# Four places for landed weight tiles and four for their high halves, in place of five and three

## The reference

```python
for i in range(DEPTH):                                   # first block
    shift, scale, gate = jnp.split(cond @ ada_w[i] + ada_b[i], 3, axis=-1)
    h = rmsnorm(x, norm_g[i]) * (1.0 + scale) + shift
    ...
    o, oc = swa_mixer(...)  # i == 0: q, k, v, gate = h @ w_in; softmax; @ w_out
    o, oc = mla_mixer(...)  # i == 1: latents, w_qb, w_kvb; softmax; @ w_out
    x = x + gate * o
for i in range(DEPTH):                                   # second block
    h = pool_mixer(...) if i % 2 == 0 else dilated_attention(...)
    x = layer_norm(DEEPNORM_ALPHA * x + h, ln_mix_g[i], ln_mix_b[i])
    x = layer_norm(DEEPNORM_ALPHA * x + sqrelu_mlp(x, mlp_w_up[i], mlp_w_down[i]), ...)
```

## Time and profile before

| | |
|---|---|
| runs of the kernel before | 3536.13, 3531.57, 6973.23 us; median 3536.13 |
| profiled execution | 3533.72 us |
| its span, from the first to the last instruction | 3531.9 us |
| granted TensorE clock, mean over the span | 0.991 |
| weights read | 580 loads, 606.72 MB on their queue |

### The profile page before, as it was taken

The page is one execution under the profiler, slowest core; times in us unless marked ns, Lnnn a source line. Parts: engine busy times, 40 slices in busy tenths (PEclk is TensorE's granted clock), DMA queues, the critical chain, the costliest instruction groups (busy, mean ns, idle before and its releaser), DMA issues.

```text
span 3531.9 us, 43704 instructions
## 1 busy us (share of the span) xinstructions
PE 3443.9 (98%) x18399; PEld 2869.4 (81%) x18399; DVE 1907.8 (54%) x2689; ACT 1437.1 (41%) x1612; POOL 139.7 (4%) x78
## 2 busy tenths in 40 slices
PE   6999999999899999999999999999999999999999
PEld 3677777777799868878888888888998788888887
DVE  2453554633677855457544554464445675445555
ACT  3213334432455543535433443353344444334432
POOL 0000000000000000005000000040000050000000
PEclk9999999999999999999999999999999999999999
DMA  8743333354332374454555555545444455555553
GB/s 324 265 155 143 131 132 120 119 204 164 116 124 109 107 269 180 167 214 167 212 194 191 191 190 191 188 176 189 182 149 162 167 188 212 197 191 189 187 195 143
DMA packets 90848, 626.09 MB, mean 177 GB/s; under 512 B 10390, under 2 KB 11415, under 8 KB 17819
## 3 DMA queue, kind: packets, MB, share of 16 engines
q1 hardware_dynamic: 85536, 606.72, 47.0%
q10 hardware_dynamic: 5116, 16.57, 1.3%
HBM read 621.15 MB, written 2.10 MB: 176 GB/s over the span
## 4 chain that ended last, share of the span: by engine, by line
PE 93%; DVE 3%; ACT 1%; issue 1%; DMA 1%; SPq 0%; DVEq 0%; ACTq 0%
PE PS L630 15%; PE PS L518 14%; PE PS L519 14%; PE PS L524 14%; PE PS L639 8%; PE PS L573 4%; PE PS L580 4%; PE PS L574 4%; PE PS L664 2%; PE PS L654 2%; DMA raw<-in_weights 1%; PE PS L791 1%; PE PS L778 1%; PE PS L736 1%; PE PS L737 1%
## 5 line engine op out<-in xcount | busy, mean ns | idle before, releaser
L1739 DVE TENSOR_TENSOR wlo<-raw,whi 128x2048 fp32r<-128x2048 f32 (+1 forms) x484 | 1099.7, 2279 | 1068.7 <-ACT whi L1243 1060.5
L1243 ACT ACTIVATE whi<-raw 128x2048 fp32r<-128x2048 f32 (+1 forms) x484 | 908.5, 1885 | 1026.2 <-PE PS L524 591.3
L630 PE MATMUL PS<-xm,whi 128*128 128x512 f32 x2384 | 569.7, 391 | 0.8 <-DVE X L2199 0.8
L630 PEld LDWEIGHTS PS<-xm,whi 128*128 128x128 f32 x2384 | 437.9, 188 | 87.2 <-issue 1.6
L518 PE MATMUL PS<-whi,hid_hi 128*128 128x512 f32 x960 | 373.8, 389 | 0.0
L519 PE MATMUL PS<-whi,hid_lo 128*128 128x512 f32 x960 | 373.5, 389 | 0.0
L639 PEld LDWEIGHTS PS<-xm,wlo 128*128 128x128 f32 x2432 | 311.8, 191 | 11.9
L639 PE MATMUL PS<-xm,wlo 128*128 128x256 f32 x2432 | 315.4, 283 | 0.0
L524 PE MATMUL PS<-wlo,hid_hi 128*128 128x512 f32 x960 | 256.6, 389 | 0.0
L524 PEld LDWEIGHTS PS<-wlo,hid_hi 128*128 128x128 f32 x960 | 180.2, 188 | 37.4
L519 PEld LDWEIGHTS PS<-whi,hid_lo 128*128 128x128 f32 x960 | 180.2, 188 | 37.3
(11 more groups left out here) (369 smaller groups left out, 5278.7 us busy)
## 6 DMA issues: line engine op xcount, KB each, us to landing
raw<-in_weights SPq DMA_DIRECT2D x560, 1024.0 KB, 4.8
lnB<-in_ln ACTq DMA_DIRECT2D x4, 2048.0 KB, 9.5
raw<-in_weights SPq DMA_DIRECT2D x8, 768.0 KB, 4.1
X<-in_x SPq DMA_DIRECT2D x4, 1024.0 KB, 8.4
X<-in_x ACTq DMA_DIRECT2D x4, 1024.0 KB, 15.9
raw<-in_weights SPq DMA_DIRECT2D x8, 512.0 KB, 3.5
raw<-in_weights SPq DMA_DIRECT2D x4, 640.0 KB, 3.7
out_x<-X SPq DMA_DIRECT2D x8, 256.0 KB, 2.1
```

The source lines that it names most:

```text
L630: mm(PS[:, banks[ch // 2] + ch % 2, :], high_of(n, slice(c * PW + ch * P, c * PW + (ch + 1) * P)), x(4 * k + c).rearrange("p s t -> p (s t ...
L1243: return f(dst, src, ACT.Copy)
L1739: v.tensor_tensor(wlo[:, ring.place[n], 0:w], raw[:, ring.place[n], 0:w], whi[:, m % NH, 0:w], ALU.subtract).then_inc(lo_done, 1)
```

## The change

Both numbers change; their sum stays 8, so that every other array of the kernel stands where it did. There are now four places for landed tiles (their loads begin when the tile four places back is done, instead of five) and four for high halves (ACT may write a high half when the split tile four back is done, instead of three). `held` becomes four as well.

```diff
-NR, NH = 5, 3
+NR, NH = 4, 4
```

## The result

| | before | four and four |
|---|---|---|
| median | 3534.68 us (22 runs) | 3542.32 us (22 runs) |
| lowest and highest | 3530.97 and 3539.62 us | 3538.36 and 3546.69 us |
| profiled execution | 3533.72 us | 3546.43 us |
| its span | 3531.9 us | 3544.6 us |

The ratio is 1.0023, 95% interval [1.0017, 1.0029]: the change costs 6.0 to 10.2 us. One of the 22 runs of before took 6973.23 us; the ratio and the highest time in the table leave it out, and without it the median of before is 3534.17. The profiled execution of the changed kernel is one of its slowest ordinary runs.

A forecast was written before the change was run, and what follows sets the result against it. PE, busy 3443.9 of 3531.9 us, was taken as the bound. Start 4.0, MLA's end 3.1, clock 4.0 and tail -0.3 summed to 10.8 on the profiled 3533.72: 3544.5 us, range 3532 to 3558.

The forecast's parts named there:

- What bounds the kernel, and the steady part: PE bounds the kernel; in the MLPs later loads stay hidden and copies come 0.6 us earlier: value 0.
- ACT's waits for landings in the attention stages: Copies may wait for loads issued some 6 us later, but ACT and DVE have room: 0, at most 6 us.
- The start: Key/value stage's first step: PE waits for late loads of tiles 12, 13, 15, 16 and 17: +4.0 us.
- Later ada tiles of the stage: The 16 ada tiles in the key/value stage's later steps land in time: 0.
- MLA's end: After sixteen ada tiles in a row, the first tile of MLA's output projection lands late: PE +3.1 us.
- The clock: PE's longer waits drop the clock to half: 2.5 us at MLA's output projection, 1.5 at the start, +4.0 us.
- The tail: Final norm: DVE finishes its first block earlier, then waits for the second: -0.3 us.
- the ada streams run dry: Rival, chance 0.14: landings over 6.8 us exhaust two places for ada tiles; 3570 us at most, 3557 in the middle.
- nothing shows: Rival, chance 0.20: PE regains the start's waits later and the projection's load is faster; 3531 to 3537 us.
- the fourth high place pays: Rival, chance 0.04: ACT's extra room returns perhaps 20 of PE's 88 idle us: 3514 us.
- slower by over 2%: Rival, chance 0.02: the chain load, high, low, use sets the pace in MLPs and projections; 3734 us.

The follow-up runs named there:

- experiment 1: Four landed and three high places, against the kernel before with five and three: 3542.22 us, ratio 1.0028.
- experiment 4: Kernel before (five and three), all loads except the first 42 and 176 to 196 delayed as with four landed places: 3534.01 us, ratio 1.0004.
- experiment 8: Three landed and four high places, three held tiles, against the kernel before with five and three: 3710.96 us, ratio 1.0502.
- experiment 3: Kernel before (five and three), only loads 176 to 196, around MLA's end, delayed as with four landed places: 3535.74 us, ratio 1.0008.
- experiment 2: Kernel before (five and three), only the first 42 loads delayed as with four landed places: 3543.15 us, ratio 1.0025.
- experiment 5: Kernel before, four ada tiles moved ahead of the key/value stage, sixteen at MLA's end spread over three heads: 3521.64 us, ratio 0.9964.
- experiment 10: Kernel before, four ada tiles ahead of the key/value stage, no pairs in its first step, sixteen at MLA's end over three heads: 3520.91 us, ratio 0.9962.

## Why the prediction was right

The change was forecast 8.4 us over the median of before as then known; it costs 7.6 us by the medians. That these two are so near is luck in part. The sum was 10.8 us, on a profiled execution of 3533.72 us; the median of before was then 3536.13, from two ordinary runs, and came down to 3534.68 later. The 10.8 is what has to be compared. Step by step:

- **What bounds the kernel, and the steady part: right.** PE 70 of 70 us, ACT's waits turned from PE to loads, three and four high places equal (experiment 1), the other 517 loads without a cost that shows (experiment 4), and even three places cover the down projections, though not quite the up projections (experiment 8). The copy came 0.63 us earlier against PE for 0.6 forecast.
- **ACT's waits for landings in the attention stages: 0, right for four places.** PE is 9.9 us later than before at 170.72 us, behind the stage, and still some 10 us later at MLA's last ada tiles. With three places (experiment 8) these stages do lose time, and that the late copies are the reason was not tried.
- **The start: +4.0, measured 5.06** (6.12 less the 1.06 of before). Tile 12 cost 1.15 for 1.2 worked out, tile 13 1.61 for 1.4, tile 15 nothing for 0.7, tile 16 0.67 for 0.4. Tile 17 was mis-sized: 2.69 us of wait where I had 1.3, since its load was issued in the stretch from 80 to 81 us and took 7.3 us to land, for 5.6 in the earlier trace rows. The landings of 4.8, 5.6 and 6.5 us were too few to go by: at this place of the changed kernel a load that goes out when the queue is empty lands in 4.7 to 4.8 us, and one behind another in 6.7 to 7.3.
- **Later ada tiles of the stage: 0, right.** None waits in the changed kernel from 94 us on.
- **MLA's end: +3.1, measured 2.7** (a pause of 3.68 for 1.21, and 0.23 at the last ada tile); 3.0 in experiment 3. The sixteen themselves landed in time, but for those 0.2 us. With the pause, the waits named on loads and this one rose by 7.9 us, for the 25.3 to 33 forecast.
- **The clock: +4.0, measured about 3.1** in this profile: at most 2.1 at the start for 1.5 (small gaps included; its one new half-speed stretch accounts for up to 1.7), and 1.0 at MLA's end for 2.5, where I had priced the pause by one of 3.75 us with a half-speed stretch of 10 us behind it; here the stretch was 3.4 us.
- **The tail: -0.3, measured -0.2**, with DVE's idle time of 2.39 us where 2.4 was forecast.

The terms as measured sum to 5.06 + 2.7 + 3.1 - 0.2 = 10.7 us, for 10.8 forecast, and the ratio says 6.0 to 10.2. The profiles of experiments 1 to 3 have the same parts at +5.05 to +5.6 (stage, where this profile has 7.15) and +4.0 (MLA's end with its clock): 9.1 to 9.6. So my sum is probably 1 to 3 us too high for the median, and which term it is stays open: with the half-speed stretches shifting from run to run, these runs cannot settle it. Nor can they settle why experiment 2 costs 8.8 us by its ratio and 11.0 by its medians, more than the 5.05 in its profile; its interval reaches down to 4.9. The parts of experiments 2 to 4 sum to 0.0037, above the 0.0023 of the change, with errors of some 0.001 each. One slip in the rivals: the worst case of the ada streams adds up to 20 + 6 + 6 + 6 = 38 us, 3572 and not 3570, which changes nothing.

Of the rivals, *nothing shows* is excluded by the interval, *the ada streams run dry* happens with three places and not with four, *the fourth high place pays* is excluded by experiment 1 and by the interval, and *slower by over 2%* by the interval; even with three places the down projections keep their pace.

## What to carry to other kernels

A place taken from a ring of loads costs nothing that shows where each tile feeds PE for longer than its part of the chain takes (here 5.44 us for 14.4 us over four places, 3.6 us), however many waits on loads then show on the copying engine; with three places, 4.8 us, the up projections already lost a little. It costs where tiles stand that feed PE for less time than they take to land, with four places here nearly only where they came in pairs, with three also where they stood alone. So look for the places where the stock is drawn down, and count landings at the two values that the trace has, for a lone load and for one behind another. Such short tiles are best put one at a time between long ones, or into a pause of PE: that was worth 12.6 and 15.3 us here (experiments 5 and 10), more than the change moved either way.

## What the runs showed of the chip that I had not expected

- **The same instructions reach the same point at three times.** The kernel of experiment 3 has the instructions and waits of the one before up to 1200 us, yet its stage begins at 59.07 us for 56.66; in experiment 2 it begins at 53.14, though PE's last wait on a load ahead of it ends within 0.4 us of theirs (38.01 us for 37.99 and 38.32). What differs is which stretches got the 1.2 GHz level. The ordinary runs of before are spread over 12 us (3528.07 to 3540.04 in one set), so one profile against another cannot show a loss of 8 us by its span, but it can by the waits of a stretch. The Trainium skill, page "TensorE: Matmul & The Clock Gate" (Part 1: The HAM clock gate), says that the same kernel has more or fewer slow matmuls from run to run, with the phase at its start; these runs agree that it varies, and none of them shows the phase.
- **Filling a pause pays for more than the pause.** Between 38.3 and 62.2 us the kernel before had two half-speed stretches; with four ada tiles in its pause (experiment 5) it has none. Windows of the same stretch, before and then of experiment 5:

```profile
38.30:62.20 23.90, 17.12 (x90) 13.63 (x94) 9.87 (x22) 11.06 (x19) 0.00 (x0) 0.64 0.48 197
```

```profile
38.30:62.20 23.90, 20.87 (x142) 14.81 (x143) 9.87 (x22) 13.75 (x22) 0.00 (x0) 1.00 0.91 376
```

  142 matmul records in place of 90, at a granted clock of 1.00 for 0.64. The stage ends 10.6 us earlier (150.22 for 160.85), of which the pause itself is 4.0 (6.76 us, now 0.62 + 1.41 + 0.75) and the two old waits on loads 1.06; the rest, about 5.6, is put down to the clock. PE worked for 6.78 and 5.54 us in the two half-speed stretches, of which up to half, 6.2 us, was lost, so the sum fits. Its five runs lie within 2.6 us of each other.
